# Choosing experts for three of five token tiles before the last tile's logits are there

## What is computed

```python
x = x + concat([o_r, o_s]) @ w_out            # retention and attention heads, merged
t = rmsnorm(x, norm2_g)
pg = softmax(t @ w_group)                     # 4 groups
g_sel = argmax(pg)
el = (t @ w_expert).reshape(-1, 4, 8)[g_sel]  # 8 experts in the chosen group
top_p, top_i = top_k(softmax(el), 2)
w = pg[g_sel] * top_p / sum(top_p)
for e in range(32):                           # SwiGLU experts, 1024 x 256 each way
    out += comb[:, e] * (silu(t @ w_gate[e]) * (t @ w_up[e])) @ w_down[e]
x = x + out
```

## Time and profile before

| | us |
|---|---|
| median of 3 runs | 558.82 (556.86 to 560.46) |
| the profiled execution, its own time | 559.13 |
| its span in the trace | 557.3 |
| PE busy | 489.2 (88%) |
| DVE busy | 267.8 (48%) |
| POOL busy | 155.8 (28%) |
| ACT busy | 132.7 (24%) |
| mean granted clock of PE | 0.951 |

### The profile page before, as it was taken

The page is one execution under the profiler, slowest core; times in us unless marked ns, Lnnn a source line. Parts: engine busy times, 40 slices in busy tenths (PEclk is TensorE's granted clock), DMA queues, the critical chain, the costliest instruction groups (busy, mean ns, idle before and its releaser), DMA issues.

```text
span 557.3 us, 7527 instructions
## 1 busy us (share of the span) xinstructions
PE 489.2 (88%) x2747; PEld 309.0 (55%) x2747; DVE 267.8 (48%) x595; ACT 132.7 (24%) x361; POOL 155.8 (28%) x279
## 2 busy tenths in 40 slices
PE   4968989899999989899992999979999789787985
PEld 3946767677776767688882754333433233333333
DVE  2869679878464475752227423223342221122535
ACT  3744455356446223222111100000000000000110
POOL 4354783042113555823004300111112210100003
PEclk9998999799999999899997699989999998898998
DMA  9430220040029703249939989999999999999997
GB/s 296 161 109 23 76 76 2 1 152 1 2 81 319 272 8 98 86 162 411 388 141 403 339 316 376 410 422 417 422 418 420 419 418 420 421 419 421 413 384 268
DMA packets 35030, 144.73 MB, mean 260 GB/s; under 512 B 5842, under 2 KB 8994, under 8 KB 23216
## 3 DMA queue, kind: packets, MB, share of 16 engines
q1 hardware_dynamic: 26320, 129.94, 59.4%
q0 software_dynamic: 4528, 9.01, 4.4%
q10 hardware_dynamic: 4144, 5.28, 2.9%
HBM read 138.16 MB, written 17.30 MB: 279 GB/s over the span
## 4 chain that ended last, share of the span: by engine, by line
PE 38%; DMA 20%; DVE 15%; SPq 11%; issue 6%; ACT 4%; POOL 1%; DVEq 0%; POOLq 0%; ACTq 0%
PE banks L1061 17%; SPq L724 7%; PE banks L1326 5%; DMA y_d<-y_sb,idx 5%; DMA w_moe_b<-in_w_up_dram 5%; DMA y_d<-rows,idx 3%; SPq L732 3%; DMA w_moe_b<-y_d 2%; DMA y_d<-x_row,idx 2%; PE banks L1416 1%; DMA y_sb<-hn_d,idx 1%; PE banks L1276 1%; PE banks L1123 1%; ACT w_hi L1604 1%; PE banks L1341 1%
## 5 line engine op out<-in xcount | busy, mean ns | idle before, releaser
L882 POOL TENSOR_TENSOR w_lo<-w_raw,w_hi 128x512 fp32r<-128x512 f32 x52 | 70.1, 1363 | 113.8 <-ACT w_hi L1604 112.4
L1326 PE MATMUL banks<-w_moe_b,xgT 128*64 128x512 f32 x224 | 68.8, 637 | 10.3 <-DMA w_moe_b<-in_w_up_dram 6.6
L1326 PE MATMUL banks<-w_moe_a,xgT 128*64 128x512 f32 x224 | 67.7, 626 | 5.6 <-DMA w_moe_a<-in_w_up_dram 5.6
L2270 DVE SCALAR_TENSOR_TENSOR glu_b<-banks,wr,glu_a 128x256 f32<-128x256 f32 x15 | 7.2, 483 | 99.5 <-ACT glu_a L1736 99.5
L1736 ACT ACTIVATE glu_a<-banks,wr 128x256 f32<-128x256 f32 x15 | 7.1, 473 | 200.1 <-PE banks L1326 185.7
L1061 PE MATMUL banks<-w_hi,xT_hi_a 128*128 128x512 f32 (+3 forms) x124 | 51.3, 414 | 2.8 <-DVE xT_lo_a L1798 2.8
L1326 PEld LDWEIGHTS banks<-w_moe_b,xgT 128*64 128x64 f32 x224 | 21.7, 145 | 49.8 <-issue 49.1
L1061 PE MATMUL banks<-w_lo,xT_hi_a 128*128 128x512 f32 (+3 forms) x124 | 49.1, 396 | 0.0
L1061 PE MATMUL banks<-w_hi,xT_lo_a 128*128 128x512 f32 (+3 forms) x124 | 48.8, 393 | 0.0
L1326 PEld LDWEIGHTS banks<-w_moe_a,xgT 128*64 128x64 f32 x224 | 21.4, 144 | 27.2 <-issue 27.0
L1061 PE MATMUL banks<-w_hi,xT_hi_b 128*128 128x512 f32 (+3 forms) x92 | 35.7, 388 | 0.4 <-issue 0.4
(11 more groups left out here) (336 smaller groups left out, 910.9 us busy)
## 6 DMA issues: line engine op xcount, KB each, us to landing
w_moe_a<-in_w_down_dram SPq DMA_DIRECT2D x20, 1024.0 KB, 21.0
w_moe_a<-in_w_gate_dram SPq DMA_DIRECT2D x16, 1024.0 KB, 12.4
w_moe_a<-in_w_up_dram SPq DMA_DIRECT2D x16, 1024.0 KB, 14.8
w_moe_b<-in_w_gate_dram SPq DMA_DIRECT2D x14, 1024.0 KB, 18.2
w_moe_b<-in_w_up_dram SPq DMA_DIRECT2D x14, 1024.0 KB, 18.3
w_moe_b<-in_w_down_dram SPq DMA_DIRECT2D x10, 1024.0 KB, 26.5
w_raw<-in_w_in_dram SPq DMA_DIRECT2D x34, 256.0 KB, 4.0
y_d<-in_consts_dram SPq DMA_DIRECT2D x9, 512.0 KB, 10.1
```

The costliest lines, as they stand in the source:

```text
L882: nc.gpsimd.tensor_tensor(w_lo[:, s, :], w_raw[:, s, :], w_hi[:, s, :].bitcast(F32), ALU.subtract).then_inc(split, 1)
L1326: l = mm(acc[64 * e:64 * e + 64, u, :].rearrange("p (m f) -> p m f", m=2), xgT[:, xu, k, 64 * e:64 * e + 64], units(at_e[e], 2)[:, :, k * ...
L2270: stt(out=glu_b[:, :], in0=acc[:, u, 0:FF], scalar=scales[0], in1=glu_a[:, :], op0=ALU.mult, op1=ALU.mult).then_inc(done, 1)
```

## The change

The choice, the ranks and the slot rows are made in two groups: the first three tiles of `ORDER` (4, 0, 1), and the last two (2, 3).

- `choose` for the first group (24 DVE steps, with a cleared `chosen` and the sum `ahead_sum` of the first three tiles) stands behind the last logits of tile 1, ahead of the scaled transpose of tile 2.
- PE makes the ranks of the first group (3 matmuls) inside the last job, ahead of its last contraction step, after waiting for `choose`.
- DVE's rank, pick and compare for the first group stand between the pieces of the last two tiles.
- Behind the last logits the same chain runs for two tiles. PE's ranks are 4 matmuls there in place of 6, and of the 10 matmuls of `find_rows` 6 can run before DVE has the last rows.
- The mean square `ms` moves from ahead of the choice to behind the last comparison (`place_of`).
- One of POOL's three memsets goes, since a part of `y_sb` serves as scratch for the first group. The tiles' columns in the router's tables are in the order of `ORDER`.

The core of the diff:

```diff
+    last = at[OUT1, ORDER[-1], 0]
+    after[last - 1].append(("choose",))
+    before[last + 1].append(("rank_in",))
+    after[last + 1].append(("rows_picked",))
+    after[last + 2].append(("rows_placed",))
...
-            for n, of in enumerate((y_sb[:, 1, 2 * NT * P - D:], x_row[DEC:, 0, :], rows[:, :, :])):
+            for n, of in enumerate((x_row[DEC:, 0, :], rows[:, :, :])):
...
+            def ranks_ahead():
+                pe.wait_ge(m_ready, 1)
+                take(RANK_BANK)
+                mm(side3[:, 0:NE * AHEAD], counting[:, 0, :], chosen[:, 0:AHEAD, :].rearrange("p t e -> p (t e)"),
+                   start=True, stop=False)
+                for s in range(1, AHEAD):
+                    l = mm(side3[:, NE * s:NE * AHEAD], counting[:, 1, :],
+                           chosen[:, 0:AHEAD - s, :].rearrange("p t e -> p (t e)"), start=False, stop=(s == AHEAD - 1))
+                l.then_inc(rank_ps, 1)
...
                 for kk in range(4 * half, 4 * half + 4):
+                    if j == NJ - 1 and kk == KD - 1:
+                        ranks_ahead()
...
+            pe.wait_ge(oh_ready, 2)
+            for k in range(2):
+                for i in range(AHEAD):
+                    find_row(0, pair_dst, row_oh, NT * k + i, k == 0 and i == 0, False)
+            pe.wait_ge(oh_ready, 3)
+            for k in range(2):
+                for i in range(AHEAD, NT):
+                    l = find_row(0, pair_dst, row_oh, NT * k + i, False, k == 1 and i == NT - 1)
+            l.then_inc(idx_ps, 1)
             pe.wait_ge(x2_add, 2 * NT)
-            find_rows(0, pair_dst, row_oh, oh_ready).then_inc(idx_ps, 1)
...
+            def choose(b):
+                dve.wait_ge(lg_ev, nth["logit", 1, ORDER[AHEAD - 1]])
+                choose_of(0, AHEAD, lot(0, AHEAD, NG, EPG), lot(96, AHEAD, EPG), lot(120, AHEAD, EPG), lot(144, AHEAD, EPG),
+                          lot(168, 2, AHEAD, EPG))
...
             dve.wait_ge(sq2, 2 * NT)
-            step(tt(ms[:, 0:NT], ssq2[:, 0, :], ssq2[:, 1, :], ALU.add))
-            step(ts(ms[:, 0:NT], ms[:, 0:NT], 1.0 / D, EPS, ALU.mult, ALU.add))
-            dve.sem_inc(ms2_rdy, 1)
...
+            place_of(AHEAD, n).then_inc(oh_ready, 1)
+            step(tt(ms[:, 0:NT], ssq2[:, 0, :], ssq2[:, 1, :], ALU.add))
+            step(ts(ms[:, 0:NT], ms[:, 0:NT], 1.0 / D, EPS, ALU.mult, ALU.add))
+            dve.sem_inc(ms2_rdy, 1)
```

More of the change, by code:

```diff
@@ L65 @@
 NJ = NT * (OUT0 + 2)
+AHEAD = 3
+RANK_BANK = 5
 SIDES = 6
@@ L1286, in _, with find_row, find_rows @@
                     does[kind](*args)
-            pe.wait_ge(m_ready, 1)
+            def find_row(c, table, oh_rows, j, start, stop):
+                return mm(found[:, c:c + 2 * NPAIR], oh_rows[:, j, :], table[:, j, :], start=start, stop=stop)
+            def find_rows(c, table, oh_rows):
+                for j in range(2 * NT):
+                    l = find_row(c, table, oh_rows, j, j == 0, j == 2 * NT - 1)
+                return l
+            pe.wait_ge(m_ready, 2)
             for b in range(SIDES):
@@ L1299, in _ @@
-            l.then_inc(rank_ps, 1)
-            def find_rows(c, table, oh_rows, half=None):
-                for j in range(2 * NT):
-                    if half is not None and j % NT == 0:
-                        pe.wait_ge(half, j // NT + 1)
-                    l = mm(found[:, c:c + 2 * NPAIR], oh_rows[:, j, :], table[:, j, :], start=(j == 0),
-                           stop=(j == 2 * NT - 1))
-                return l
+            mm(side3[:, NE * AHEAD:NE * (NT + 1)].rearrange("p (t e) -> p t e", e=NE), counting[:, 1, :],
+               ahead_sum[:, :].unsqueeze(1).to_broadcast([P, NT + 1 - AHEAD, NE]), start=False, stop=False)
@@ new lines, in _ @@
+            for s in range(1, NT + 1 - AHEAD):
+                l = mm(side3[:, NE * (AHEAD + s):NE * (NT + 1)], counting[:, 1, :],
+                       chosen[:, AHEAD:NT + 1 - s, :].rearrange("p t e -> p (t e)"), start=False, stop=(s == NT - AHEAD))
+            l.then_inc(rank_ps, 1)
+            pe.wait_ge(oh_ready, 2)
[3 more added lines that the diff above has]
+            pe.wait_ge(oh_ready, 3)
@@ new lines, in choose_of, with col, wide, iota_n @@
+            def choose_of(lo, n, r32, cand, el, el2, oh_e):
+                of = slice(lo, lo + n)
+                gl, groups = logits[:, of, 0:NG], oh_g[:, of, :]
+                def col(c):
+                    return small[:, c + lo:c + lo + n]
+                def wide(ap, w):
+                    return ap.unsqueeze(2).to_broadcast([P, n, w])
+                def iota_n(w):
+                    return small[:, 100:100 + w].unsqueeze(1).to_broadcast([P, n, w])
+                def lowest(out, c, w):
+                    step(red(col(120), c, AX_X, ALU.min))
+                    step(tt(out, c, wide(col(120), w), ALU.is_equal))
+                step(red(col(30), gl, AX_X, ALU.max))
+                step(tt(r4[:, of, :], gl, wide(col(30), NG), ALU.subtract))
+                step(stt(out=cand[:, :, 0:NG], in0=r4[:, of, :], scalar=0.0, in1=iota_n(NG), op0=ALU.is_equal, op1=ALU.mult))
+                lowest(groups, cand[:, :, 0:NG], NG)
+                e4 = logits[:, of, NG:].rearrange("p t (g e) -> p t g e", g=NG)
+                step(tt(r32, e4, groups.unsqueeze(3).to_broadcast([P, n, NG, EPG]), ALU.mult))
+                step(red(el, r32.rearrange("p t g e -> p t e g"), AX_X, ALU.add))
+                step(red(col(35), el, AX_X, ALU.max))
+                step(tt(el, el, wide(col(35), EPG), ALU.subtract))
+                step(stt(out=cand, in0=el, scalar=0.0, in1=iota_n(EPG), op0=ALU.is_equal, op1=ALU.mult))
+                lowest(oh_e[:, 0], cand, EPG)
+                step(stt(out=el2, in0=oh_e[:, 0], scalar=NEG, in1=el, op0=ALU.mult, op1=ALU.add))
+                step(red(col(40), el2, AX_X, ALU.max))
+                step(tt(cand, el2, wide(col(40), EPG), ALU.is_equal))
+                step(tt(cand, cand, iota_n(EPG), ALU.mult))
+                lowest(oh_e[:, 1], cand, EPG)
+                if lo == 0:
+                    dve.wait_ge(half_used, OUT1)
+                    step(nc.vector.memset(chosen[:, AHEAD:, :].bitcast(F32), 0.0))
+                for k in range(2):
+                    step(tt(oh[:, k, of].rearrange("p t (g e) -> p t g e", g=NG),
+                            oh_e[:, k].unsqueeze(2).to_broadcast([P, n, NG, EPG]),
+                            groups.unsqueeze(3).to_broadcast([P, n, NG, EPG]), ALU.mult))
+                if lo == 0:
+                    step(nc.vector.memset(oh[DEC:, :, 0, :], 0.0))
+                step(tt(chosen[:, of, :], oh[:, 0, of], oh[:, 1, of], ALU.add))
+                if lo == 0:
+                    two, by_tile = scratch[:, 504:504 + NE], [chosen[:, i, :].bitcast(F32) for i in range(AHEAD)]
+                    step(tt(two, by_tile[0], by_tile[1], ALU.add))
+                    step(tt(ahead_sum[:, :], two, by_tile[2], ALU.add))
+                dve.sem_inc(m_ready, 1)
@@ L2179, in _ @@
[L2179 to L2182 removed]
+            n = NT - AHEAD
+            choose_of(AHEAD, n, glu_b[:, 0:n * NE].rearrange("p (t g e) -> p t g e", t=n, g=NG), cand[:, 0:n, :],
+                      el[:, 0:n, :], el2[:, 0:n, :],
+                      actT[:, :, :].rearrange("p a n -> p (a n)")[:, 0:2 * n * EPG].rearrange("p (k t e) -> p k t e", k=2, t=n))
```

113 lines of the change are left out of this document (53 added, 60 removed).

## The result

The changed kernel takes 561.53 us (median of 20 runs, 558.41 to 563.65) against 558.21 us for the kernel before (20 runs, 556.25 to 560.93). The recorded ratio of the two sets is 1.0047, with a 95% interval of 1.0029 to 1.0064: 2.6 us more (1.6 to 3.6). The two medians alone lie further apart, 3.3 us. By the bound of 1% set in the prediction that counts as no change, though the interval leaves out 1. The time lies 1.1 us above the 560.4 that was forecast.

A forecast was written before the change was run, and what follows sets the result against it. It took the weight stream, held up at its start by PE's work and the first gather, as the bound; 0.0 (gather) plus 1.6 us (clock) on 559.13 gave 560.7, set to 560.4 for the median, range 557.0 to 563.2 us.

The forecast's parts named there:

- What bounds: Up to 321 us, every us on the first gather or PE's work counts fully; other engines' work counts nothing.
- The choice ahead and PE's stall: First group's choice ends at 292.05 us, PE stalls 0.9 us in the last job, last logits come 1.65 us late.
- The second choice and idx: Behind the last logits: second choice takes some 4.65 us, ends at 302.05; idx at about 306.3 for 308.82 us.
- The mean square: POOL's root, now late, ends at 309.05 us ahead of the first gather, which goes out at 309.95: change 0.0.
- PE's clock: A 2.1 us PE gap ahead of the second find_rows lowers the clock: 1.6 us lost, between 0 and 6.1.
- (A): Gap ahead of the second find_rows costs nothing, unread matmuls raise the clock sooner: 558.5 us, chance 0.22.
- (B): Saving at idx reaches the gather, which goes out at 307.3 to 308 us: 556.5 us, chance 0.12.
- (C): PE between 310 and 321 us at clock 0.50 deep into the first pair: 564 us with 5 us lost, chance 0.14.
- (D): Work ahead comes later, PE's stall in the last job is 3 us rather than 0.9: 562.5 us, chance 0.06.

The follow-up runs named there:

- e5: The kernel before with four unread matmuls in place of nine ahead of the second find_rows: ratio 1.0040 to the kernel before.
- e3: The changed kernel with fourteen unread matmuls in place of nine: ratio 1.0011 to the kernel before.
- e2: The changed kernel with the first group's ranks made behind the last projection job instead of inside it: ratio 1.0033 to the kernel before.
- e1: The changed kernel with the mean square made behind the first group's comparison, ahead of the last logits: ratio 1.0023 to the kernel before.
- e4: The kernel before with only the mean square moved, from ahead of the choice to behind row_oh: ratio 1.0033 to the kernel before.
- e9: The kernel before, ungrouped, with the 1 MB load behind the first gather's landing and twelve unread matmuls: ratio 0.9994 to the kernel before.
- e6: The kernel before with the load of pair 0's first down matrix (1 MB) issued behind the first gather's landing: ratio 0.9964 to the kernel before.
- e7: e1 with the 1 MB load of pair 0's first down matrix moved behind the first gather's landing: ratio 0.9972 to the kernel before.
- e11: e8 with the mean square late again, behind the last comparison as in the changed kernel: ratio 1.0040 to the kernel before.
- e8: e7 with twelve unread matmuls in place of nine: ratio 0.9944 to the kernel before.
- e12: e8 run a second time, with nothing changed: ratio 0.9977 to the kernel before.

## Why the prediction was right, point by point

**What bounds.** That every us up to pair 0's first half passes on to the end is borne out in size: e5 moves that half's end by 1.9 us and the time by 2.2, and over the fourteen executions that end moves by 5.5 us (32.19 to 37.68) while the time behind it stays within 2 us in all but e3.

**The choice ahead and PE's stall.** Forecast: `chosen` from 286.35 to 292.05, thus at 5.94 on the common scale, and a stall of 0.9 us. Measured: 5.97 and 0.76. The last logits were to come at 11.09 and came at 11.22. The step named PE's stall, though, and e2 shows that DVE, not that stall, sets them. SP's loads behind the job went out 1.4 us late as forecast (7.42 for 6.05), and costing that at nothing held: over the 26 us from tile 1's logits the transfers average 361 GB/s in both kernels.

**The second choice and idx.** Forecast 15.94 and 20.2, measured 16.02 and 20.26. The rule of 0.16 us for a step and 1 ns for an element, read from the earlier trace rows, held to 0.1 us, and with it that the fixed part, paid twice, takes back what smaller tiles save.

**The mean square.** Forecast: root from 19.54 to 22.94 and the gather at 23.84 with ends of -0.6 and +0.4. Measured: 19.57 to 22.88, and 23.57. Right in mechanism, place and size for when the gather goes out, and e1 and e4 show it from both sides. But the step took it that the gather's issue alone decides when the rows land. With the gather out anywhere from 22.18 to 25.07 the rows landed between 28.66 and 29.09 (before, after, e1 to e5). Two things decide: the gather needs some 4.1 us of its own (4.1 to 4.2 us in e9 and e6, 4.0 in e4), and it does not land before the weights queued ahead of it are through. Of the 4.80 us of the earlier trace rows, 4.1 to 4.2 are its own and the rest is the queue. The result hid this, because the forecast change was 0.0 on either reading; that part of the hit is luck.

By the Trainium skill (DMA: Bandwidth & Descriptors, Issuing engines are not separate DMA queues) transfers started by SP and by POOL run on the same sixteen engines and interleave. The traces agree: share 0.99 to 1.00 until 314 us in e1, where POOL's gather took 6.6 us, and 4.9 us when 1 MB of SP's is taken from in front of it (e7).

**PE's clock.** Right in place and in kind (PE at the lower level for longer), short in size, and its reason, the gap, not shown. The gap was forecast at 2.1 us and measured at 1.78; the term was 1.6 us, between 0 and 6.1. The trace shows 1.66 us more in the sum (10.38 for 8.72), of which 1.13 reach the end of the half, since the gap let `find_rows` start 0.15 us sooner and less slack was left before the transposes. Over 20 runs the whole change costs 2.6 us (1.6 to 3.6). The other terms were forecast at nothing, and the profiled execution shows nothing of them at the landing (28.71 for 28.66), so **the clock term of 1.6 us is the one that was short, by about 1 us**, though 1.6 lies just at the edge of the interval.

What carries the cost is shown from two sides: taking five unread matmuls from the kernel before costs 0.40% (e5), and giving five to the changed kernel leaves 0.11% of its 0.47% (e3). But both edits change the gap and the work ahead of it together, and in the changed kernel the clock fell 1.8 us behind the gap, with PE busy. That the gap itself brings the clock down is argued, not shown.

By the Trainium skill (TensorE: Matmul & The Clock Gate, HAM oscillation) a wait between short bursts lets the next burst start cold. That section of the Trainium skill tells of longer waits than the 1.2 to 1.8 us here. These traces don't show its rule for such gaps: the changed kernel's burst starts at 1.00 behind 1.78 us and so does e11's behind 1.66 us, while e7 is at 0.50 without a gap.

**The rivals.** (A), the gap costs nothing, fell on the time. Its reason came true, the clock rose 1.5 us sooner, but it fell sooner as well. (B), the saving at `idx` arrives, fell on the root as argued, and would have fallen on the queue too: e1 takes the root out of the way, moves the gather by 1.4 us and the landing not at all. (C), slower by the clock, is nearest in kind, at half its price: 3.7 us of pair 0 ran at 0.50. But its mark, 0.50 when the second `find_rows` starts, was met in e2 and e5 and not in the changed kernel's profiled execution. (D), the work ahead is late, fell: 0.76 us.

**Could the grouping pay?** No run shows that it does. With the root early, the 1 MB load behind the gather and twelve unread matmuls it stands at 0.9944 and 0.9977 (e8, e12), where the same two edits without it give 0.9994 (e9). Those intervals overlap. And the kernel without grouping, with the load alone moved and its nine unread matmuls kept, stands at 0.9964 (e6), between e8 and e12. So the gain of these kernels may be that of the load alone. The change alone could win nothing: its 2.45 us at `idx` ended first behind POOL, then behind the queue, and left a gap on PE.

**Open.** What makes the clock rise and fall where it does (low in e7 without a gap, high in e11's profiled execution behind one); what e1's remaining 0.23% is; what of e6's gain is the landing and what the clock; and what moves tile 1's logits by up to 4 us between executions.

## What to carry to other kernels

Before a wait is shortened, read what the transfer behind it waits for: an issue-to-landing time beside a DMA share of 1.00 can hold a wait in a queue on top of the transfer's own length, and only that wait is shortened by moving what is queued ahead. Its own length is read where the engines are idle. When a step leaves the path, look at what it covered: here a root that moved into POOL's busy stretch, and a row of unread matmuls that no longer reached the work behind it. When a kernel has unread matmuls ahead of a stretch that matters, their number is tried again with every change that moves the work around them. And before a gain is put down to a change, it is set beside the kernel without that change and with each of the other edits alone.
